# Rotating by partition-shifted ScalarE copies instead of permutation products

## The chip, the cores and the metric

The kernel runs on one core of a Trainium2 chip. The metric is device time in microseconds (us), lower is better. Before the change it takes 2796.73 us, the median of three runs (2792.71 to 2798.84).

## What is computed

A two-layer backbone with four parallel token mixers. It works on 512 latent and 256 context tokens, 1024 features, everything in float32. Each layer projects the normalised tokens to heads of four mixers (retention, gated linear attention, grouped-query attention, differential attention). Retention and grouped-query attention rotate their queries and keys, heads of 64 features, on the latent tokens only:

```
def apply_rope(x, cos, sin):
    h = x.shape[-1] // 2
    x1, x2 = x[..., :h], x[..., h:]
    return jnp.concatenate([x1 * cos - x2 * sin, x1 * sin + x2 * cos], axis=-1)

# retention:      q, k = apply_rope(z['ret_q']), apply_rope(z['ret_k']) * scale
# grouped-query:  q = apply_rope(rms_norm(z['gqa_q'], q_norm)); k = apply_rope(rms_norm(z['gqa_k'], k_norm))
```

The query heads of grouped-query attention are four, its key heads two. Differential attention rotates too, in heads of 32, and is not touched here.

## The kernel before

Features lie on the partitions and tokens along the free dimension. A "feature tile" is 128 features (two heads of 64) by up to 768 tokens; retention has four of them (queries 0 and 1, keys 2 and 3), grouped-query attention three (key tile 2 first, then query tiles 0 and 1). In layer 1 only the 512 latent tokens have queries. Values come from "token projections", with tokens on the partitions, two column tiles at a time for retention and one for grouped-query attention.

Each engine has its own list of instructions, written out by hand in order and joined by semaphores; `room` gives PSUM banks to products and makes TensorE (PE) wait until ScalarE (ACT) or VectorE (DVE) has freed them. A weight tile comes through a ring of four buffers; GpSimd (POOL) splits it into a high and a low part (L1284, L1287), and every product is three matmuls (L506 to L508 for feature and gate tiles, L547 to L549 for token projections).

Around a rotation this happens. PE projects feature tile n into banks (0,1) or (2,3), in turns. ACT copies it out to `q[:, n]` (`out_of_psum`, L1469, for retention; `queries_out`, L1510, with the norm weight, for the queries of grouped-query attention; L1633 for its keys), which frees the banks. PE then multiplies the tile by the 128x128 matrix `perm64`, which swaps the halves of each head and changes one sign (`rotate`, L668); that product is in plain float32 and shows as two matmul records. DVE multiplies the product by the sine table, the tile by the cosine table, and adds (`turn`, L1978, L1979, L1981). Retention has four rotations in each layer: two after the first token projection, two after the second. The first token projection of either mixer uses banks 0, 1 and 2, so it waits until ACT has freed the last feature tile. In grouped-query attention ACT also squares each tile for its norm (L1519) and that is what frees the banks; PE sums the squares (L653, L657), ACT takes the root (L1527, L1530), and DVE normalises the key tile (L1965 reciprocal, L1967) before it is rotated. At the end of that stage PE multiplies the rotated key tile by `swap`, which exchanges its two heads (`swapped_keys`, L924), and ACT copies the result to `q[:, 3]`, because query and key must lie on the same partitions.

In the retention stage of layer 0 ACT and DVE also build four "strips" of decays, one after each feature tile in ACT's order (`strip_exponentials`, L1388 to L1392). Strip h+1 begins on DVE only after strip h has ended there (L2014 to L2017, then L2006 and L2007), and each needs ACT's four exponentials in the middle.

Of the kernel before, what the change touches and what calls it, by code (L numbers as in the profile page):

```python
# [15 lines left out]
P = 128  # L16
# [3 lines left out]
T = LAT + CTX  # L20
# [28 lines left out]
SMALL = [("ident", P), ("ones", P), ("sum64", P), ("sum32", P), ("perm64", P), ("perm32", P),  # L49
         ("tri", 2 * P), ("rest", 2 * P), ("two", P), ("swap", P)]  # L50
# [4 lines left out]
def constants():  # L55

    f = np.float32
    j, i = np.arange(P)[:, None], np.arange(P)[None, :]
    c = {}
    c["ident"] = (j == i).astype(f)  # L60
    c["two"] = 2 * c["ident"]
    c["swap"] = (j == (i + P // 2) % P).astype(f)
    c["ones"] = np.full((P, P), 1.0 / D, f)
    for d in (64, 32):
        c[f"sum{d}"] = (j // d == i // d).astype(f) / d
        half = d // 2
        first = i % d < half
        c[f"perm{d}"] = (((j == i + half) & first) * -1.0 + ((j == i - half) & ~first) * 1.0).astype(f)
# [19 lines left out]
    rope = np.concatenate([*ret, *axial(64), *axial(32)], 1).astype(f)  # L88
    p = np.arange(P)[:, None]
    e = np.arange(7 * P)[None, :]  # L90
# [141 lines left out]
def bass_hybrid_backbone(nc, A, out, marks):  # L232
# [6 lines left out]
    with ctx:  # L239
# [215 lines left out]

        def query_roots(l, b, n):
            return q_scale[:, 0, n, 0:(4 if b == "dif" else 2) * NQ[l]]
# [24 lines left out]
        def _(pe):  # L482
# [177 lines left out]
            def rotate(l, b, n):  # L660
                key = ("rope", l, b, n)
                for s, c in room(key, 6 if n != feature_order(b)[-1] else 3 if b == "gqa" else 4):
# [254 lines left out]
            def swapped_keys(l):  # L917

                key = ("swap", l)
                for s, c in room(key, 4, 5):  # L920
                    pe.wait_ge(s, c)
                pe.wait_ge(*at(("turned", l, "gqa", 2)))
                for x, y in segs(T):
                    mm = pe.matmul(psum(key)[:, x:y], K["swap"], q[:, 2, x:y], start=True, stop=True)  # L924
                mm.then_inc(*up("pe_full", ("full", key)))

# [39 lines left out]
            for l in range(DEPTH):  # L966
# [27 lines left out]
                for b in ORDER:  # L994
                    nf, nt = len(BR[b]["feat"]), len(BR[b]["tok"])
                    lag = 4 if b == "ret" else 2
                    for j in range(nf + lag):
# [23 lines left out]
                        if b != "gla" and lag <= j < nf + lag - 1:  # L1021
                            rotate(l, b, feature_order(b)[j - lag])
# [326 lines left out]
        def _(act):  # L1349
# [156 lines left out]

            def queries_out(l, b, n):

                act.wait_ge(*at(("full", ("f", l, b, n))))
                act.activation(q[:, n, 0:W[l]], psum(("f", l, b, n))[:, 0:W[l]], ACT.Identity, scale=colv(l, 1, VB_QN + (0 if b == "gqa" else 2)),  # L1510
                               bias=zero).then_inc(*up("queries", ("turnable", l, b, n)))
# [107 lines left out]
            for l in range(DEPTH):  # L1619
                if l == 0:  # L1620
                    norm(l, 1)
                for b in ORDER:
                    nf, nt = len(BR[b]["feat"]), len(BR[b]["tok"])
                    for j in range(nf + nt):
                        if j < nf:
# [3 lines left out]
                            if b in ("gqa", "dif") and is_q(b, n):  # L1629
                                queries_out(l, b, n)  # L1630
                            elif b in ("gqa", "dif"):
# [38 lines left out]
                    if b == "gqa":  # L1670
                        out_of_psum(q[:, 3, :], ("swap", l), T)
# [77 lines left out]
        def _(dve):  # L1749
# [201 lines left out]
            def prep_tiles(l, b):  # L1951
# [17 lines left out]

                def turn(n):  # L1970
                    key = ("rope", l, b, n)
                    dve.wait_ge(*at(("free", ("f", l, b, n))))
                    dve.wait_ge(*at(("full", key)))
                    if b == "ret" and n == 0:
                        dve.wait_ge(*at(("rope_in", l)))
                    z = q[:, n, 0:LAT]
                    part = prep[:, 1, 0:LAT] if b == "ret" else prob[:, 0, 0, 0:LAT]
# [5 lines left out]
                if b == "ret":  # L1983
                    for n in range(tiles):
                        turn(n)
                    return
                keys, queries = feature_order(b)[:tiles - 2], feature_order(b)[tiles - 2:]
                for n in keys:
# [413 lines left out]
```

## Time and profile before

| what | value |
|---|---|
| median of three runs | 2796.73 us |
| span of the profiled execution | 2781.7 us |
| PE busy | 2638.2 us, 95% of the span |
| DVE, ACT, POOL busy | 47%, 26%, 53% |
| the chain that ended last | PE 83%, DVE 9%, ACT 3%, DMA 2% |
| mean granted TensorE clock | 0.981 of full speed |

The span is that of one execution under the profiler, from its first to its last instruction; what the device time has beyond it is start and end of the launch. The rows of a timeline give the start, the duration, the engine, the line of the kernel, the operation and its operands; "[1.30 <-DVE arena L1967]" says that the engine stood idle for 1.30 us before the row, until that instruction released it.

### The profile page before, as it was taken

To read this page: it belongs to the slowest core of one execution; us is meant where nothing else is said; L and a number is where in the kernel's file an instruction comes from. 1 tells how busy PE (TensorE), PEld (TensorE's weight loads), DVE (VectorE), ACT (ScalarE), POOL (GpSimd) and SP (SyncE) were. 2 spreads that over 40 slices of the span, in tenths; PEclk is the share of its full clock that TensorE was granted. 3 is DMA by queue.
4 is the path that set the end of the run, shared out by engine and by line. 5 is a ranking of instruction groups with operands and counts; after the bars stand their busy time and mean duration, and the time that the engine had idled before them with its cause. 6 is when DMAs were issued, how large, how long until landed. Compare 5 with 4: busy or idle time off the path is not lost.

```text
span 2781.7 us, 38375 instructions
## 1 busy us (share of the span) xinstructions
PE 2638.2 (95%) x15708; PEld 2172.5 (78%) x15708; DVE 1313.6 (47%) x1835; ACT 711.3 (26%) x1214; POOL 1465.5 (53%) x1375
## 2 busy tenths in 40 slices
PE   5999989998999999999999999998999889999999
PEld 2788878776877878888878888886777667888877
DVE  3622066534476847555573352317644667511231
ACT  4411143222254621111120121133321455211110
POOL 2543437521423526666669426545733436488886
PEclk9999989999999999999999999999999999999999
DMA  7522412211411834444433363221212218433322
GB/s 262 159 61 77 128 42 67 81 47 33 114 54 45 273 110 124 122 122 122 123 106 109 118 205 86 84 57 54 73 52 52 61 57 249 115 99 99 96 80 82
DMA packets 378083, 285.19 MB, mean 103 GB/s; under 512 B 10245, under 2 KB 338601, under 8 KB 377398
## 3 DMA queue, kind: packets, MB, share of 16 engines
q1 hardware_dynamic: 375680, 279.91, 33.7%
q8 instruction: 125, 2.05, 0.3%
q10 hardware_dynamic: 1622, 2.75, 0.3%
q14 instruction: 48, 0.39, 0.0%
q0 software_dynamic: 608, 0.09, 0.0%
HBM read 253.35 MB, written 29.36 MB: 102 GB/s over the span
## 4 chain that ended last, share of the span: by engine, by line
PE 83%; DVE 9%; ACT 3%; DMA 2%; issue 1%; POOL 1%; ACTq 0%; SPq 0%; DVEq 0%; POOLq 0%
PE ps L506 18%; PE ps L507 17%; PE ps L508 17%; PE ps L1137 3%; PE ps L678 3%; PE ps L547 2%; PE ps L549 2%; PE ps L548 2%; PE ps L1083 2%; DVE ffl L2328 2%; PE ps L762 2%; PE ps L782 1%; PE ps L889 1%; PE ps L640 1%; PE ps L709 1%
## 5 line engine op out<-in xcount | busy, mean ns | idle before, releaser
L1284 POOL TENSOR_TENSOR w_hi<-ring,tiny 128x512 fp32r<-128x512 f32 x484 | 535.5, 1106 | 1045.8 <-PE ps L508 612.2
L1287 POOL TENSOR_TENSOR w_lo<-ring,w_hi 128x512 fp32r<-128x512 f32 (+1 forms) x572 | 798.7, 1398 | 95.7 <-ACT w_hi L1489 57.5
L506 PE MATMUL ps<-hh,w_hi 128*128 128x512 f32 (+1 forms) x2288 | 836.7, 366 | 11.8 <-DVE hl L1906 9.8
L507 PE MATMUL ps<-hl,w_hi 128*128 128x512 f32 (+1 forms) x2288 | 812.9, 355 | 0.0
L508 PE MATMUL ps<-hh,w_lo 128*128 128x512 f32 (+1 forms) x2288 | 811.3, 355 | 0.0
L506 PEld LDWEIGHTS ps<-hh,w_hi 128*128 128x128 f32 x2288 | 438.6, 192 | 109.9 <-issue 29.1
L508 PEld LDWEIGHTS ps<-hh,w_lo 128*128 128x128 f32 x2288 | 438.4, 192 | 61.7
L507 PEld LDWEIGHTS ps<-hl,w_hi 128*128 128x128 f32 x2288 | 439.3, 192 | 57.5 <-issue 1.9
L547 PE MATMUL ps<-w_hi,hh 128*128 128x256 f32 (+1 forms) x544 | 156.8, 288 | 4.6 <-POOL w_lo L1287 2.5
L1557 ACT ACTIVATE arena<-ps,tiny,vec 128x768 f32<-128x768 f32 (+1 forms) x120 | 108.6, 905 | 197.5 <-DVE tiny L2064 197.4
L548 PE MATMUL ps<-w_lo,hh 128*128 128x256 f32 (+1 forms) x544 | 154.4, 284 | 0.0
L549 PE MATMUL ps<-w_hi,hl 128*128 128x256 f32 (+1 forms) x544 | 154.4, 284 | 0.0
L506 PE MATMUL ps<-ffh,w_hi 128*128 128x512 f32 x352 | 141.5, 402 | 11.6 <-DVE ffl L2328 11.5
L2337 DVE SCALAR_TENSOR_TENSOR arena<-ps,vec,arena 128x511 f32<-128x511 f32 x66 | 43.6, 661 | 224.0 <-ACT arena L1723 223.3
L1723 ACT ACTIVATE arena<-ps,vec 128x768 f32<-128x768 f32 (+1 forms) x44 | 39.0, 887 | 428.8 <-PE ps L508 428.8
L1834 DVE SCALAR_TENSOR_TENSOR rope<-ring,tiny,rope 128x1024 f32<-128x1024 f32 x84 | 146.4, 1783 | 0.7
L508 PE MATMUL ps<-ffh,w_lo 128*128 128x512 f32 x352 | 137.2, 390 | 0.0
L507 PE MATMUL ps<-ffl,w_hi 128*128 128x512 f32 x352 | 137.2, 390 | 0.0
L1469 ACT ACTIVATE arena<-ps 128x512 f32<-128x512 f32 (+3 forms) x116 | 65.1, 563 | 232.2 <-PE ps L508 231.1
L2063 DVE TENSOR_REDUCE tiny<-ps 128x1 f32<-128x768 f32 (+1 forms) x120 | 101.4, 845 | 44.3 <-PE ps L746 29.7
L1329 POOL TENSOR_TENSOR arena<-arena 128x128 f32<-128x128 f32 x140 | 60.8, 434 | 114.1 <-DVE xT L2166 68.4
L547 PEld LDWEIGHTS ps<-w_hi,hh 128*128 128x128 f32 x544 | 105.7, 194 | 10.4 <-issue 4.0
(256 smaller groups left out, 3837.0 us busy)
## 6 DMA issues: line engine op xcount, KB each, us to landing
ring<-in_w_in SPq DMA_DIRECT2D x118, 512.0 KB, 4.0
ring<-in_w_mod SPq DMA_DIRECT2D x96, 512.0 KB, 3.9
ring<-in_w_up SPq DMA_DIRECT2D x88, 512.0 KB, 4.1
ring<-in_w_down SPq DMA_DIRECT2D x48, 512.0 KB, 4.0
ring<-in_w_out SPq DMA_DIRECT2D x32, 512.0 KB, 4.1
logits<-arena SPq DMA_DIRECT2D x32, 384.0 KB, 2.3
arena<-logits SPq DMA_DIRECT2D x32, 384.0 KB, 4.5
ring<-in_w_down SPq DMA_DIRECT2D x24, 384.0 KB, 3.4
```

What stands on the lines that cost most here:

```text
L506: pe.matmul(acc, wh[:, offset + k], hi[:, n, x:y], start=n == 0, stop=False)
L507: pe.matmul(acc, wh[:, offset + k], lo[:, n, x:y], start=False, stop=False)
L508: mm = pe.matmul(acc, wl[:, offset + k], hi[:, n, x:y], start=False, stop=n == whole - 1)
L547: pe.matmul(to, hh[:, n, ts], wh[:, :, k], start=n == 0 and bank_begins, stop=False)
L548: pe.matmul(to, hh[:, n, ts], wl[:, :, k], start=False, stop=False)
L549: mm = pe.matmul(to, hl[:, n, ts], wh[:, :, k], start=False, stop=n == KT - 1 and bank_ends)
L678: mm = pe.matmul(psum(("oT", l, b, t))[64 * s:64 * s + 64, P * c:P * c + P], vt, pt[s][:, m], start=m == key_tiles(t)[0], stop=m == NT - 1)
L1284: pool.tensor_tensor(wh[:, 0:count], w, one[:].unsqueeze(2).to_broadcast([P, count, P]), ALU.mult).then_inc(*up("w_lead", ("lead", key, j)))
L1287: pool.tensor_tensor(wl[:, 0:count], w, wh[:, 0:count].bitcast(F32), ALU.subtract).then_inc(*up("w_split", ("split", key, j)))
L1557: act.activation(prob[:, h % 2, m, lo:T], psum(key)[:, lo:T], ACT.Exp, scale=scale, bias=nmx[:, c:c + 1], accum_out=rsum[t % 2][:, 4 * m + ...
L1834: ins = dve.scalar_tensor_tensor(out=mod_sum[:, s], in0=w, scalar=cs[:, s, k:k + 1], in1=mod_sum[:, s], op0=ALU.mult, op1=ALU.add)
L2063: link(dve.tensor_reduce(nmx[:, c:c + 1], acc[:, lo:T], AX, ALU.max))
```

## The change

The four rotations of retention and the three of grouped-query attention, in both layers, no longer use PE. ACT, when it takes a feature tile out of PSUM, writes it a second time with the 32-partition halves of each head exchanged: four activations of 32 partitions by 512 tokens, read from PSUM at one partition offset and written to SBUF at another. The sign goes into the sine table. For grouped-query attention the key tile is rotated before it is normalised (the root is the same for all features of a head), and its norm weight is applied by ACT. The head swap of the keys becomes two copies of 64 partitions by 768 tokens on ACT. The constant matrices `perm64` and `swap` are no longer loaded. Differential attention stays as it was.

```
+        def other_halves(l, b, n):
+            if b == "gqa":
+                return prob[:, n // 2, n % 2, 0:LAT]
+            if n == 3:
+                return q[:, 4, 0:LAT]
+            return (prep if l == 0 else pt_r).rearrange("p b t -> p (b t)")[:, n * LAT:(n + 1) * LAT]
...
             def rotate(l, b, n):
-                if b == "ret":
-                    pe.wait_ge(*at(("free", ("f", l, b, n))))
-                else:
-                    pe.wait_ge(*at(("turnable", l, b, n)))
-                pe.matmul(psum(key)[:, 0:LAT], K["perm32" if b == "dif" else "perm64"], q[:, n, 0:LAT],
+                pe.wait_ge(*at(("turnable", l, b, n)))
+                pe.matmul(psum(key)[:, 0:LAT], K["perm32"], q[:, n, 0:LAT],
                           start=True, stop=True).then_inc(*up("pe_full", ("full", key)))
...
-                        if b != "gla" and lag <= j < nf + lag - 1:
+                        if b == "dif" and lag <= j < nf + lag - 1:
                             rotate(l, b, feature_order(b)[j - lag])
...
-                    if b == "gqa":
-                        swapped_keys(l)
+                    if b == "dif":
+                        rotate(l, b, feature_order(b)[-1])
                     if b in ("gqa", "dif"):
-                        rotate(l, b, feature_order(b)[-1])
...
                     if b == "ret":
-                        rotate(l, b, nf - 1)
...
+            def halves_out(l, b, n, scale):
+                for to in range(0, P, 32):
+                    src = to ^ 32
+                    rows = slice(src, src + 32)
+                    ins = act.activation(other_halves(l, b, n)[to:to + 32], psum(("f", l, b, n))[rows, 0:LAT], ACT.Identity,
+                                         scale=scale[rows], bias=zero[rows])
+                return ins
...
             def queries_out(l, b, n):
...
+                ins = act.activation(q[:, n, 0:w], psum(("f", l, b, n))[:, 0:w], ACT.Identity, scale=column, bias=zero)
+                if b == "gqa":
+                    ins = halves_out(l, b, n, column)
+                ins.then_inc(*up("queries", ("turnable", l, b, n)))
+
+            def features_out(l, n):
+                key = ("f", l, "ret", n)
+                act.wait_ge(*at(("full", key)))
+                w = W[l] if is_q("ret", n) else T
+                act.activation(q[:, n, 0:w], psum(key)[:, 0:w], ACT.Copy)
+                halves_out(l, "ret", n, one).then_inc(*up("act_free", ("free", key)))
...
                     if b == "gqa":
-                        out_of_psum(q[:, 3, :], ("swap", l), T)
+                        act.wait_ge(*at(("turned", l, b, 2)))
+                        act.activation(q[0:64, 3, :], q[64:128, 2, :], ACT.Copy)
+                        act.activation(q[64:128, 3, :], q[0:64, 2, :], ACT.Copy).then_inc(*up("act_free", ("free", ("swap", l))))
...
+                def turn_halves(n):
+                    dve.wait_ge(*at(("free", ("f", l, b, n)) if b == "ret" else ("turnable", l, b, n)))
+                    if b == "ret" and n == 0:
+                        dve.wait_ge(*at(("rope_in", l)))
+                    z, part = q[:, n, 0:LAT], other_halves(l, b, n)
+                    dve.tensor_tensor(part, part, rope[:, cos_sin + 1], ALU.mult)
+                    link(dve.tensor_tensor(z, z, rope[:, cos_sin], ALU.mult))
+                    ins = dve.tensor_tensor(z, z, part, ALU.add)
+                    if b == "ret" or is_q(b, n):
+                        step(ins, "turned", ("turned", l, b, n))
+                        return
+                    link(ins)
+                    z, roots = q[:, n, 0:T], key_roots(n)
+                    dve.wait_ge(*at(("free", ("qkn", l, b, n))))
+                    link(dve.reciprocal(roots, roots))
+                    step(dve.tensor_tensor(z, z, roots, ALU.mult), "turned", ("turned", l, b, n))
```

## Rows read from the trace of the kernel before

**Rows 1.** The page, part 1: busy time, share of the span, instructions, by engine.

```profile
PE 2638.2 (95%) x15708; PEld 2172.5 (78%) x15708; DVE 1313.6 (47%) x1835; ACT 711.3 (26%) x1214; POOL 1465.5 (53%) x1375
```

**Rows 2.** Groups by shape, PE: count | busy us, mean ns | idle before.

```profile
L668 PE MATMUL ps<-arena,small 128*128 128x512 f32 x44 | 25.4, 661 | 9.2 <-DVE arena L1967 4.9 <-DVE arena L1978 1.8 <-ACT modv L1423 1.4
```

**Rows 3.** Timeline of PE, grouped-query stage of layer 0.

```profile
561.39 0.30 PE L547 MATMUL ps<-w_hi,hh 128*128 128x128 f32 x1
...
577.49 1.45 PE L653 MATMUL ps<-small,arena 128*128 128x2 f32 x12
578.80 1.10 PE L668 MATMUL ps<-arena,small 128*128 128x512 f32 x2
579.74 1.47 PE L938 MATMUL ps<-small,arena 128*128 128x128 f32 x12
581.05 1.46 PE L924 MATMUL ps<-arena,small 128*128 128x512 f32 x4
582.34 1.02 PE L668 MATMUL ps<-arena,small 128*128 128x512 f32 x2
...
588.76 1.56 PE L746 MATMUL ps<-arena 64*128 64x512 f32 x8
```

**Rows 4.** Groups by shape, ACT.

```profile
L1510 ACT ACTIVATE arena<-ps,tiny,vec 128x512 f32<-128x512 f32 x4 | 3.1, 777 | 17.5 <-PE ps L508 17.5
L1519 ACT ACTIVATE arena<-ps 128x512 f32<-128x512 f32 x4 | 2.3, 587 | 0.0
L1469 ACT ACTIVATE arena<-ps 32x768 f32<-32x768 f32 x2 | 1.6, 799 | 15.5 <-PE ps L508 15.5
```

**Rows 5.** Timeline of ACT, grouped-query stage of layer 0.

```profile
560.32 0.27 ACT L1527 ACTIVATE vec<-ps,tiny 128x12 f32<-128x12 f32 x1 [0.52 <-PE ps L653]
560.49 0.80 ACT L1519 ACTIVATE arena<-ps 128x768 f32<-128x768 f32 x1
```

**Rows 6.** Timeline of ACT, retention stage of layer 0.

```profile
94.89 0.95 ACT L1388 ACTIVATE arena<-arena 128x896 f32<-128x896 f32 x1 [3.40 <-DVE arena L2007]
...
108.60 0.91 ACT L1392 ACTIVATE arena<-dist,tiny 128x640 f32<-128x640 f32 x1
109.76 0.81 ACT L1469 ACTIVATE arena<-ps 128x768 f32<-128x768 f32 x1 [0.25 <-PE ps L508]
```

**Rows 7.** Timeline of PE, retention stage of layer 0.

```profile
112.63 0.35 PE L547 MATMUL ps<-w_hi,hh 128*128 128x256 f32 x1 [1.91 <-POOL w_lo L1287]
...
129.97 0.95 PE L577 MATMUL ps<-tiny,arena 128*128 128x2 f32 x8
...
166.52 0.71 PE L709 MATMUL ps<-arena 64*128 64x128 f32 x8
```

**Rows 8.** Timeline of PE, retention stage of layer 1.

```profile
1694.23 0.36 PE L547 MATMUL ps<-w_hi,hh 128*128 128x256 f32 x1 [0.95 <-ACT arena L1469]
...
1711.58 1.02 PE L668 MATMUL ps<-arena,small 128*128 128x512 f32 x2
...
1734.17 1.61 PE L709 MATMUL ps<-arena 64*128 64x128 f32 x24 [0.33 <-issue]
```

**Rows 9.** Timeline of PE, grouped-query stage of layer 1.

```profile
2014.77 0.95 PE L653 MATMUL ps<-small,arena 128*128 128x2 f32 x8
2017.02 1.10 PE L668 MATMUL ps<-arena,small 128*128 128x512 f32 x2 [1.30 <-DVE arena L1967]
```

**Rows 10.** Groups by shape, DVE.

```profile
L1965 DVE RECIPROCAL arena<-arena 128x768 f32<-128x768 f32 x6 | 29.7, 4953 | 45.4 <-ACT arena L1530 45.4
L1979 DVE TENSOR_TENSOR arena<-arena,rope 128x512 f32<-128x512 f32 x22 | 21.6, 981 | 0.0
```

**Rows 11.** Windows around the first rotations: length, PE, PEld, DVE, ACT, POOL busy, PEclk, DMA share, GB/s.

```profile
131.00:134.40 3.40, 1.85 (x2) 0.30 (x2) 0.00 (x0) 1.30 (x5) 3.24 (x4) 0.74 0.18 25
134.40:137.80 3.40, 2.64 (x6) 1.61 (x7) 2.42 (x4) 0.00 (x0) 0.54 (x1) 0.50 0.94 258
137.80:141.20 3.40, 3.40 (x24) 3.40 (x23) 1.55 (x3) 0.00 (x0) 0.00 (x0) 0.76 0.11 30
```

More of the change, by code:

```diff
@@ L48 @@
 VB_CW, VB_C, VB_QN, VB_ROWS = 0, 3 * FT, 3 * FT + 2 * KT, 3 * FT + 2 * KT + 4
-SMALL = [("ident", P), ("ones", P), ("sum64", P), ("sum32", P), ("perm64", P), ("perm32", P),
-         ("tri", 2 * P), ("rest", 2 * P), ("two", P), ("swap", P)]
+SMALL = [("ident", P), ("ones", P), ("sum64", P), ("sum32", P), ("perm32", P),
+         ("tri", 2 * P), ("rest", 2 * P), ("two", P)]
 W = {l: (T if l < DEPTH - 1 else LAT) for l in range(DEPTH)}
@@ L65, in constants @@
         c[f"sum{d}"] = (j // d == i // d).astype(f) / d
-        half = d // 2
-        first = i % d < half
-        c[f"perm{d}"] = (((j == i + half) & first) * -1.0 + ((j == i - half) & ~first) * 1.0).astype(f)
+    first = i % 32 < 16
+    c["perm32"] = (((j == i + 16) & first) * -1.0 + ((j == i - 16) & ~first) * 1.0).astype(f)
     c["tri"] = np.concatenate([(j <= i), (j >= i)], 1).astype(f) / 16
@@ L86, in axial @@
                                    (tok % GRID_W).astype(f)[:, None] * fr], -1), dim)
-    rope = np.concatenate([*ret, *axial(64), *axial(32)], 1).astype(f)
     p = np.arange(P)[:, None]
+    sign = np.where(p % 64 < 32, -1, 1).astype(f)
+    cos64, sin64 = axial(64)
+    rope = np.concatenate([ret[0], sign * ret[1], cos64, sign * sin64, *axial(32)], 1).astype(f)
     e = np.arange(7 * P)[None, :]
@@ L661, in rotate @@
                 key = ("rope", l, b, n)
-                for s, c in room(key, 6 if n != feature_order(b)[-1] else 3 if b == "gqa" else 4):
+                for s, c in room(key, 6 if n != feature_order(b)[-1] else 4):
                     pe.wait_ge(s, c)
-                if b == "ret":
-                    pe.wait_ge(*at(("free", ("f", l, b, n))))
-                else:
-                    pe.wait_ge(*at(("turnable", l, b, n)))
-                pe.matmul(psum(key)[:, 0:LAT], K["perm32" if b == "dif" else "perm64"], q[:, n, 0:LAT],
+                pe.wait_ge(*at(("turnable", l, b, n)))
+                pe.matmul(psum(key)[:, 0:LAT], K["perm32"], q[:, n, 0:LAT],
                           start=True, stop=True).then_inc(*up("pe_full", ("full", key)))
@@ L915, in gla @@
                     mm.then_inc(*up("pe_full", ("full", key)))
[L917 to L925, printed above, removed]
             def turn_outputs(l, b):
@@ L1505, in outputs_out @@
                     *up("act_free", ("free", key)))
+            def halves_out(l, b, n, scale):
[5 more added lines that the diff above has]
+                return ins
             def queries_out(l, b, n):
+                w = W[l] if is_q(b, n) else T
+                column = colv(l, 1, VB_QN + (0 if b == "gqa" else 2) + (0 if is_q(b, n) else 1))
                 act.wait_ge(*at(("full", ("f", l, b, n))))
-                act.activation(q[:, n, 0:W[l]], psum(("f", l, b, n))[:, 0:W[l]], ACT.Identity, scale=colv(l, 1, VB_QN + (0 if b == "gqa" else 2)),
-                               bias=zero).then_inc(*up("queries", ("turnable", l, b, n)))
+                ins = act.activation(q[:, n, 0:w], psum(("f", l, b, n))[:, 0:w], ACT.Identity, scale=column, bias=zero)
[8 more added lines that the diff above has]
+                halves_out(l, "ret", n, one).then_inc(*up("act_free", ("free", key)))
             def query_squares(l, b, n):
@@ L1628, in _ @@
                             M = 32 if BR[b]["feat"][n] == 2048 else P
-                            if b in ("gqa", "dif") and is_q(b, n):
+                            if b == "ret":
+                                features_out(l, n)
+                            elif b == "gqa" or (b == "dif" and is_q(b, n)):
                                 queries_out(l, b, n)
-                            elif b in ("gqa", "dif"):
+                            elif b == "dif":
                                 act.wait_ge(*at(("full", ("f", l, b, n))))
@@ L1973, in turn @@
                     dve.wait_ge(*at(("full", key)))
-                    if b == "ret" and n == 0:
-                        dve.wait_ge(*at(("rope_in", l)))
                     z = q[:, n, 0:LAT]
-                    part = prep[:, 1, 0:LAT] if b == "ret" else prob[:, 0, 0, 0:LAT]
+                    part = prob[:, 0, 0, 0:LAT]
                     dve.tensor_tensor(part, psum(key)[:, 0:LAT], rope[:, cos_sin + 1], ALU.mult).then_inc(*up("dve_free", ("free", key)))
@@ L1984, in prep_tiles @@
                     for n in range(tiles):
-                        turn(n)
+                        turn_halves(n)
                     return
                 keys, queries = feature_order(b)[:tiles - 2], feature_order(b)[tiles - 2:]
-                for n in keys:
+                for n in keys if b == "dif" else ():
                     if n != keys[0]:
```

4 lines of the change are left out of this document (3 added, 1 removed).

## The prediction

> **What bounds the kernel now.** I read the page first: PE is busy 95% of the span and the other engines at most 53% [rows 1], so work taken from PE is worth its time wherever PE goes on at once, and work given to ACT costs only where PE waits for ACT. Averages don't say where that is. So I read next PE's groups by shape, to count what goes, and then, for each of the four places where rotations stand (retention and grouped-query attention, layers 0 and 1), the timelines of PE, ACT and DVE side by side. There the reader should look at the row with which PE starts the first token projection: it needs the banks of the last feature tile, which ACT frees. In layer 1's retention PE already waits 0.95 us for exactly that ACT copy [rows 8]; in the grouped-query stage of layer 0 PE starts at 561.39, when ACT's last square (560.49 plus 0.80) has just ended [rows 3, 5]. Everything the change adds on ACT stands in front of that row. I take the sum against the profiled span of 2781.7 us; the median of the runs is 15.0 us more, and I leave those 15 as they are.
>
> **What goes from PE.** The rotations are 22, two records each [rows 2]; 8 of them are differential attention's and stay, 14 go. One takes 0.94 us from its start to the next product's (578.80 to 579.74), a key swap 1.29 (581.05 to 582.34) [rows 3]. That is 14 x 0.94 + 2 x 1.29 = 15.7 us (the second swap is taken at the same price). The waits around the rotations go with them.
>
> **What ACT gets.** One shifted copy is 512 tokens with a scale and a bias read from SBUF, the form of L1510: 777 ns against 587 for a plain one of that width [rows 4]. That it moves only 32 partitions saves nothing: a 32x768 copy takes 799 ns [rows 4]. An activation starts about 0.1 us before the one ahead ends (560.32 plus 0.27, next at 560.49) [rows 5]. So each copy costs 0.68 to 0.69 us in a queue and four cost 2.75 us per feature tile. The bounds: 0.49 us (the plain form, overlapped) and, if moving between partitions has a price that no row shows, anything above; that is a rival below. The same 2.75 us stand behind all 14 tiles, 38 us of ACT, but they are hidden behind the next projection of the same mixer, except after the last tile.
>
> **Retention, layer 0.** Two delays add up. The strips are a chain between ACT and DVE: ACT idles 3.40 us for DVE before the second strip's exponentials [rows 6], and DVE in turn waits for ACT, so four copies put in front of the first strip move the whole chain by 2.75. The third strip's last exponential ends at 109.51 now [rows 6], then at 112.3. Only then comes the last feature tile: one copy (0.71) and four halves (2.8) end at 115.8, and PE starts at 115.9 and not at 112.63 [rows 7], where it now waits for POOL's split: 3.3 us lost. After that come the gains. From the end of the first token projection to the first scores it is now 129.97 to 166.52, 36.55 us [rows 7]. What is left of it: the modulation product 0.95; the second projection, 144 matmuls like the first (17.34 us, so 0.120 each); the gate tile, 24 matmuls of 512 and 24 of 256 columns, 72 such units, 8.7. Together 27.0, gain 9.6. More than the four rotations (3.8), since their waits and a low clock go too (below). Net 6.3.
>
> **Retention, layer 1.** The last tile's halves add 2.75 to PE's wait. From 1711.58 to 1734.17 it is 22.6 us [rows 8]; left are 96 matmuls (11.6), 24 of 512 (5.8) and 0.33 of issue, 17.7: gain 4.9. Net 2.1.
>
> **Grouped-query, layer 0.** ACT's chain between the last query tile and its square has 0.52 us of waiting for PE in it [rows 5], which absorbs part of the 2.75: PE starts the token projection 2.2 later than 561.39. Behind it two rotations and the swap go, 0.94 + 1.29 + 0.94 = 3.2. Net 1.0.
>
> **Grouped-query, layer 1.** PE waits 1.30 us for DVE to normalise the keys, then rotates (2017.02), so the projection starts at 2017.96 [rows 9]. Afterwards ACT sets it: full at 2014.77 plus 0.2, copy 0.69, halves 2.75, root 0.17, square 0.59, handoff 0.1: 2019.3. Lost 1.3, gained the same 3.2. Net 1.9.
>
> **What costs nothing, and its cover.** DVE keeps three operations per tile (up to about 1 us each [rows 10]); it can do them while PE is still at the second token projection, which is over 11 us long, and before they stood behind PE. The key tile's reciprocal (4.95 us [rows 10]) moves behind the rotation and starts some 3 us later, but the scores come only at 588.76 [rows 3], more than 25 us after. The swap by ACT, two copies of 768 (about 1.6 us), stands behind the copies of the previous mixer's outputs; its cover is the half gate tile that PE does before the scores (2.7 us in layer 1, 5.4 in layer 0). By my count layer 1 has only some 0.2 us to spare, so up to 1 us could show there. In retention the gate tile's second half of weights is split by POOL only after the projection's last product; with the rotations gone, PE gets there 2.7 us after that product, and POOL's two operations are next to be late. No DMA is moved. SP stores gate logits after ACT's copies; in layer 1 these stand behind two tiles' halves and come some 5 us later, and the load queued behind the store waits with it, but that weight is used over 15 us later. The smaller table of constants is not what the start waits for: nothing, at most 0.5 us of gain.
>
> The four nets make 6.3 + 2.1 + 1.0 + 1.9 = 11.3 us.
>
> **The clock.** Around the first two rotations the granted clock is 0.50 for about 6.8 us (0.74, 0.50, 0.76 in three windows), after PE had done only small products and waits; that is 1.2 instead of 2.4 GHz. PE was busy 1.85, 2.64 and 3.40 us in them [rows 11], so it cost about 0.8 + 1.3 + 0.8 = 2.9 us. The change takes this away (it is inside the 9.6), but makes four new stretches in which PE has little or nothing: about 5 us before the projection in layer 0's retention, 4 in layer 1's, 5.6 and 4.5 us of tiny sums and waiting in the grouped-query stages. I count on the two long ones, at 2.2 each, between the 2.9 of all three windows and the 1.3 of the middle one alone: 4.4 us lost. The two ends are kept for the range.
>
> Forecast: 11.3 - 4.4 = 6.9 us, so the span about 2775 and the time 2790.
>
> **The rivals.**
> *All new gaps lower the clock, or ACT's delays are a little longer.* Four times 2.2 to 2.9 us is 8.8 to 11.6, which leaves 2.5 or nothing: 2794 to 2797. The Trainium skill, TensorE: Matmul & The Clock Gate, HAM oscillation, tells of a loop whose every idle gap throttled the engine again and was paid for each time; by it this rival would be the likeliest and the time about 2795. The trace agrees as far as one such gap goes, with PEclk at 0.50 behind it [rows 11]. For the rival: the gaps of 4 us are not much shorter than the others; the swap and POOL are close. Against it: PE waits of 1.9 us (112.63 [rows 7]) show no lowered clock in the trace.
> *No gap lowers it.* Gain 11 to 12.7, with copies at 0.6 us: 2784 to 2786. For it: PE works at full density up to three of the four. Against it: rows 11.
> *A shifted copy costs much more than a straight one.* The place is the same row in the four stages. With price p the lost time is 8p (two tiles in layer 0's retention) plus 4p three times, less about 4.4 absorbed: 20p - 4.4, against 20.9 won (9.6 + 4.9 + 3.2 + 3.2). It is slower by over 5.6 us once 20p is over 30.9, p over 1.55 us, 2.2 times the row's. At 1.7 us: 2805. Nothing in the trace moves data between partitions on ACT, so only the absence of a row speaks for it.
> *The change does not do what it says:* PE's idle time takes the place of the products fully, with everything else equal: 2796.7. Against it: the four gains lie behind the first token projection, where ACT has little to do.
>
> **How the numbers follow.** 0.2%, 5.6 us, is what a measurement of this kernel can tell from no change. Chances: forecast (two gaps, or one or three) 0.45; no gap 0.15; all gaps or longer ACT delays 0.25; no gain at all 0.06; expensive copies 0.09. The forecast's own range is 2787 to 2793, which crosses the limit at 2791.1; I give three quarters of it to faster. Faster: 0.34 + 0.15 + a little of the rest, 0.51. Slower: 0.09. Same: 0.40. Range for 8 in 10: from the no-gap case, 2784, to the end of the all-gaps case, 2797.
>
> **What would show it.** PE busy down by about 16 us; no L668 in retention and grouped-query stages; ACT busy up by 38 to 45. Four halves at 0.78 us each behind each tile's copy. PE's wait before the first token projection about 5, 3.7, 3.4 and 3.6 us, its releaser ACT. PEclk at 0.5 after the first and the third. Wrong if the halves take over 1 us, if PE waits elsewhere (for `turned`, the swap or POOL before the gate tile), or if the time saved in these stages is given back in the gated linear attention that follows.

## The result: slower, by two stages at half clock

The changed kernel takes 2808.9 us (median of 22 runs, 2802.7 to 2815.4), the kernel before 2798.9 in the same comparison (22 runs, 2773.4 to 2816.7): a ratio of 1.0046, 95% interval 1.0027 to 1.0065, so 10 us slower, beyond the 0.2% that the prediction took as its limit. Forecast were 2790 and a range from 2784 to 2797. The profiled execution has a span of 2813.4 us and a time of 2815.3; the first and last 1.9 us are all that lies around the span. So before's profiled span of 2781.7 stands for a run of some 2783.6, not for the median 15 us above it.

The page of the changed kernel, part 1, against [rows 1]:

```profile
PE 2662.6 (95%) x15672; PEld 2205.4 (78%) x15672; DVE 1318.3 (47%) x1835; ACT 759.5 (27%) x1272; POOL 1469.3 (52%) x1375
```

ACT has 48 us more in 58 more instructions. PE has 36 instructions fewer and is busy 24 us *longer*. That can't come from less work; something makes products slower. Groups by shape of the changed kernel show which (after the bar: busy us, mean ns, idle before):

```profile
L555 PE MATMUL ps<-w_hi,hh 128*128 128x256 f32 x448 | 130.3, 291 | 8.7 <-ACT arena L1505 7.2 <-ACT arena L1462 0.9 <-POOL w_lo L1280 0.5
...
L555 PE MATMUL ps<-w_hi,hh 128*128 128x128 f32 x96 | 39.9, 416 | 7.8 <-ACT arena L1533 7.8
```

The 128-column products of this line, which are grouped-query attention's token projection, take 416 ns on average, longer than those of twice the width. The timelines of PE and ACT in layer 0 show how it comes to that, against [rows 3, 5] (L555 to L557 are the old L547 to L549, L661 the old L653, L1533 the square, L1505 the shifted halves):

```profile
553.60 0.95 PE L585 MATMUL ps<-tiny,arena 128*128 128x2 f32 x8
554.41 1.48 PE L661 MATMUL ps<-small,arena 128*128 128x2 f32 x12
559.64 0.44 PE L555 MATMUL ps<-w_hi,hh 128*128 128x128 f32 x1 [3.75 <-ACT arena L1533]
...
590.39 2.66 PE L661 MATMUL ps<-small,arena 128*128 128x2 f32 x12
...
595.36 0.70 PE L514 MATMUL ps<-hh,w_hi 128*128 128x512 f32 x1
...
601.23 1.56 PE L751 MATMUL ps<-arena 64*128 64x512 f32 x8
```

```profile
553.80 0.99 ACT L1514 ACTIVATE arena<-ps,tiny,vec 128x768 f32<-128x768 f32 x1 [4.46 <-PE ps L516]
554.80 3.12 ACT L1505 ACTIVATE arena<-ps,tiny,vec 32x512 f32<-32x512 f32 x4
...
558.70 0.84 ACT L1533 ACTIVATE arena<-ps 128x768 f32<-128x768 f32 x1
```

ACT is where the prediction put it: copy, four halves, root, square, then PE may start. The wait is 3.75 us. But from 559.64 to 590.39 the projection takes 30.75 us, where before it took 16.1 [rows 3]. Windows over the same stretch (length, then PE, PEld, DVE, ACT, POOL busy, PEclk, DMA share, GB/s):

```profile
547.00:555.00 8.00, 8.00 (x56) 7.31 (x54) 6.19 (x3) 3.47 (x6) 6.14 (x6) 1.00 0.81 213
555.00:560.00 5.00, 1.25 (x10) 1.19 (x11) 4.45 (x7) 4.48 (x10) 2.17 (x2) 0.83 0.31 78
560.00:565.00 5.00, 5.00 (x25) 5.00 (x25) 1.61 (x3) 0.00 (x0) 0.00 (x0) 0.50 0.09 27
...
580.00:590.00 10.00, 10.00 (x49) 10.00 (x48) 0.00 (x0) 0.00 (x0) 0.00 (x0) 0.50 0.00 0
590.00:600.00 10.00, 10.00 (x46) 9.22 (x46) 0.58 (x3) 4.41 (x6) 2.31 (x2) 0.71 0.21 54
600.00:606.00 6.00, 6.00 (x40) 4.68 (x39) 2.25 (x4) 3.08 (x5) 1.36 (x2) 1.00 0.00 0
```

After 5 us in which PE worked 1.25, the granted clock is 0.50 (1.2 GHz), and it stays there through 30 us in which PE is busy without a pause, with the other engines idle. It is at 1.00 again only with the 512-column gate products behind, half a microsecond after their first at 595.36, so the small sums between them ran at half clock too (2.66 us against 1.45 in [rows 3]). Layer 1 is the same, by its timeline:

```profile
2027.23 0.95 PE L661 MATMUL ps<-small,arena 128*128 128x2 f32 x8
2032.23 0.44 PE L555 MATMUL ps<-w_hi,hh 128*128 128x128 f32 x1 [4.05 <-ACT arena L1533]
...
2062.98 1.81 PE L661 MATMUL ps<-small,arena 128*128 128x2 f32 x8
...
2071.10 1.56 PE L751 MATMUL ps<-arena 64*128 64x512 f32 x8
```

The two retention stages, for [rows 7, 8], PE's timeline (L714 are the scores):

```profile
114.22 0.35 PE L555 MATMUL ps<-w_hi,hh 128*128 128x256 f32 x1 [3.11 <-ACT arena L1505]
...
133.05 0.95 PE L585 MATMUL ps<-tiny,arena 128*128 128x2 f32 x8
...
159.75 0.82 PE L714 MATMUL ps<-arena 64*128 64x128 f32 x9
...
1709.57 0.55 PE L555 MATMUL ps<-w_hi,hh 128*128 128x256 f32 x1 [4.08 <-ACT arena L1505]
...
1729.48 0.28 PE L555 MATMUL ps<-w_hi,hh 128*128 128x256 f32 x1
...
1746.66 1.61 PE L714 MATMUL ps<-arena 64*128 64x128 f32 x24
```

And three rows more of the kernel before, PE's timeline: where layer 0's grouped-query projections end, where layer 1's token projection ends (the same sums as 2062.98 above), and its first scores:

```profile
557.99 0.95 PE L577 MATMUL ps<-tiny,arena 128*128 128x2 f32 x8
...
2033.98 1.00 PE L653 MATMUL ps<-small,arena 128*128 128x2 f32 x8
...
2041.66 1.56 PE L746 MATMUL ps<-arena 64*128 64x512 f32 x8
```

Step by step against before: layer 0's retention is 6.8 us earlier at its first scores (159.75, [rows 7] 166.52); at the last tile's sums of layer 0's grouped-query stage 4.4 of it are left (553.60 against 557.99); at its first scores the kernel is 12.5 late (601.23, [rows 3] 588.76), so this stage lost 16.9. Layer 1's retention ends 12.5 late, as it began (1746.66, [rows 8] 1734.17), and layer 1's grouped-query stage loses 17.0 again (29.4 us late behind it, by the same instructions in both traces). Two losses of 17 against one gain of 7. Of the 2.4 us that went between the two stages of layer 0, 1.6 lie before 366.13 (360.94 now), where a dip of the clock that both kernels have is longer in this run: the granted clock is 0.89 over the last 47.7 us before that row, 0.93 over the same work before. The remaining 0.8, and the 2.3 between 29.4 and the 31.7 us by which the spans differ, weren't traced.

Within the two grouped-query stages the 17 us split up like this. PE starts the token projection 2.6 us later in layer 0 and 1.9 in layer 1, counted from the last feature product. The projection loses 14.7 in each. Behind it, where the rotations and the swap have gone, layer 0 gains 0.4 (590.39 to 601.23, before 577.49 to 588.76) and layer 1 loses 0.4 (2062.98 to 2071.10, before 2033.98 to 2041.66).

### The profile page after: what moved, and what is told of

Read it like the earlier page. It is cut to its first block and busy times, and to the rows that moved or that the text cites. A ratio compares the mean times of both kernels' runs of the same rounds, so it can differ in the third digit from the quotient of the medians.

```text
span 2813.4 us, 38328 instructions
## 1 busy us (share of the span) xinstructions
PE 2662.6 (95%) x15672; PEld 2205.4 (78%) x15672; DVE 1318.3 (47%) x1835; ACT 759.5 (27%) x1272; POOL 1469.3 (52%) x1375
## 3 DMA queue, kind: packets, MB, share of 16 engines
q10 hardware_dynamic: 1622, 2.75, 0.3%
## 5 line engine op out<-in xcount | busy, mean ns | idle before, releaser
L514 PE MATMUL ps<-hh,w_hi 128*128 128x512 f32 (+1 forms) x2288 | 836.3, 366 | 12.5 <-DVE hl L1924 10.4
L555 PE MATMUL ps<-w_hi,hh 128*128 128x256 f32 (+1 forms) x544 | 170.2, 313 | 16.5 <-ACT arena L1533 8.0
L556 PE MATMUL ps<-w_lo,hh 128*128 128x256 f32 (+1 forms) x544 | 169.2, 311 | 0.0
L557 PE MATMUL ps<-w_hi,hl 128*128 128x256 f32 (+1 forms) x544 | 169.2, 311 | 0.0
L555 PEld LDWEIGHTS ps<-w_hi,hh 128*128 128x128 f32 x544 | 120.6, 222 | 20.7 <-ACT arena L1533 8.9
L556 PEld LDWEIGHTS ps<-w_lo,hh 128*128 128x128 f32 x544 | 120.6, 222 | 0.2 <-issue 0.2
```

Source lines behind the costliest of these rows:

```text
L514: pe.matmul(acc, wh[:, offset + k], hi[:, n, x:y], start=n == 0, stop=False)
L555: pe.matmul(to, hh[:, n, ts], wh[:, :, k], start=n == 0 and bank_begins, stop=False)
L556: pe.matmul(to, hh[:, n, ts], wl[:, :, k], start=False, stop=False)
L557: mm = pe.matmul(to, hl[:, n, ts], wh[:, :, k], start=False, stop=n == KT - 1 and bank_ends)
```

## The experiments

Twelve kernels ran. Theory A says that the low clock, once there, stays through the stream of 128-column products and costs 30.8 - 16.1 = 14.7 us per layer (the stream alone, without what runs at half clock behind it); theory B that the wait or ACT's and DVE's work beside it is the cost. Times are medians, and the ratio is to the kernel before on the same chip.

**Take the wait away.** The projection's 768 columns need two of the three banks that it asks for.

```diff
-for s, n in room(("tt", l, b, pair[0]), first, first + 1, first + 2):
+for s, n in room(("tt", l, b, pair[0]), *range(first, first + (3 if len(pair) == 2 else 2))):
```

> The changed kernel, but grouped-query attention's token projection (768 columns, so two banks) asks for two banks of the accumulator instead of three. Those two belong to the first feature tile, long read, so PE no longer waits for ACT after the last query tile (3.75 us in layer 0, 4.05 in layer 1 in the changed kernel's trace). Theory A (the wait lowers the clock, and the stream of 144 products of 128 columns then runs to its end at 0.50): PE starts at once after the small sums, the projection takes 16.1 us instead of 30.8 in both layers, and the kernel gains 2 x (3.8 + 14.7) = 37 us, or about 30 where the before kernel's level is shared by other losses: 2772 to 2780 us. Theory B (the wait is the whole cost, the slow projection has another cause, such as ACT's or DVE's traffic beside it): gain 7.8 us, about 2801, and the pitch stays at 0.21 us.

2778.8 us (2762.4 to 2788.8), ratio 0.9944 (0.9914 to 0.9974): 30 us under the changed kernel, far beyond theory B's 7.8. But its profile holds a surprise. Windows of layer 0, where PE had no wait at all (2.2 us of small sums from 547.06, then the projection from 549.22):

```profile
549.50:551.90 2.40, 2.40 (x24) 2.40 (x23) 2.37 (x3) 2.35 (x7) 1.22 (x1) 1.00 0.03 4
551.90:555.00 3.10, 3.10 (x17) 3.10 (x17) 2.56 (x7) 1.10 (x4) 0.00 (x0) 0.51 0.62 166
555.00:570.00 15.00, 15.00 (x72) 15.00 (x72) 0.10 (x1) 0.00 (x0) 2.31 (x2) 0.50 0.00 1
```

The clock falls just the same and stays down, but it falls inside the stream, 2.7 us after its start. In layer 1 of the same run it does not fall. So without the wait the clock is lost in some cases and not in others, which would explain the spread of 26 us. Whether the two-column products ahead of the stream bring it down or the stream itself does, this run can't tell; moving the sums (below) asks that.

**Keep PE busy in the wait.** Four plain products of 512 columns, whose output nothing reads, ahead of the wait:

```diff
+if b == "gqa" and pair[0] < 2:
+    for s, n in room(("fill", l), 6):
+        pe.wait_ge(s, n)
+    for i in range(4):
+        mm = pe.matmul(psum(("fill", l))[:, 0:512], K["ones"], rope[:, 4, 0:512], start=True, stop=True)
+    mm.then_inc(*up("pe_full", ("free", ("fill", l))))
 for s, n in room(("tt", l, b, pair[0]), first, first + 1, first + 2):
     pe.wait_ge(s, n)
```

> The changed kernel with four extra plain products of 512 columns per layer (0.94 us each by the rotations' rows), put ahead of the wait for ACT in front of grouped-query attention's token projection; their output is never read. The wait's end is set by ACT as before. Theory A (PE's idling in the wait lowers the clock and the projection keeps it low): PE is busy through the 3.8 us, the clock stays at 1.00, the projection takes 16.1 us: gain 2 x 14.7 = 29 us, 2778 to 2784 us, though PE does 7.5 us more work. Theory B (the wait, or ACT's and DVE's work beside the projection, is the cost): no gain, 2809 us or up to 4 more.

2775.5 us (2769.4 to 2780.9), ratio 0.9931 (0.9903 to 0.9959): 33 us less than the changed kernel for 7.5 us more work on the bounding engine. The expectation that the clock stays at 1.00 did not hold in layer 0. It fell, but the extra products took the dip, and the projection ran at full clock:

```profile
549.50:555.00 5.50, 5.50 (x14) 2.46 (x13) 4.92 (x9) 3.60 (x9) 1.38 (x1) 0.69 0.38 95
555.00:563.00 8.00, 8.00 (x74) 8.00 (x74) 0.26 (x1) 0.00 (x0) 0.11 (x1) 1.00 0.01 2
```

In layer 1 the clock stayed at 1.00 through the projection, as expected. Theory B can't have this: ACT's and DVE's work and what PE waits for are unchanged.

**The same products behind the wait** (the six lines moved under the room's wait).

> The same four extra products per layer, now behind the wait and in front of the token projection. The wait stays, and the clock falls in it as before. Theory A, in its form that only the 128-column products fail to raise the clock: the 512-column ones raise it within their own 4 to 7.5 us, the projection then takes 16.1 us: net gain per layer 14.7 less 3.8 to 7.5, so 14 to 22 us in all, 2787 to 2795. If a low clock lasts whatever PE does then, or if the cause lies beside PE: 8 to 15 us slower than the changed kernel, 2817 to 2824.

2787.8 us (2775.7 to 2790.5), ratio 0.9968 (0.9933 to 1.0003), 21 us less than the changed kernel. Timeline of PE and windows in layer 0:

```profile
558.48 5.97 PE L548 MATMUL ps<-rope,small 128*128 128x512 f32 x8 [3.74 <-ACT arena L1539]
563.88 0.62 PE L561 MATMUL ps<-w_hi,hh 128*128 128x128 f32 x1
```

```profile
554.50:558.50 4.00, 0.26 (x4) 0.20 (x3) 3.44 (x7) 3.82 (x9) 1.58 (x1) 0.72 0.31 66
558.50:564.00 5.50, 5.50 (x9) 2.42 (x9) 1.95 (x3) 0.00 (x0) 0.00 (x0) 0.58 0.16 47
564.00:572.00 8.00, 8.00 (x72) 7.76 (x71) 0.00 (x0) 0.00 (x0) 0.00 (x0) 1.00 0.01 2
```

The wait is the changed kernel's (3.74 us) and the clock falls in it. Four wide products at low clock cost 5.4 us and end the dip; 144 narrow ones don't. The wait alone is not the loss. With the clock kept, the stretch behind the projection takes 8.2 us in layer 0 and 4.9 in layer 1 of this run, 3.0 and 2.8 less than before (11.3 and 7.7), where the changed kernel gained 0.4 and lost 0.4. So half clock behind the projection costs that kernel a further 2.6 and 3.2 us.

**Is it the width?** Retention's token projection has 256-column products and came back to full clock after its own wait of 4.08 us. Here its first one is issued in halves of the width.

```diff
+for c in range(2):
+    half = to[:, c * P:(c + 1) * P]
+    pe.matmul(half, hh[:, n, ts], wh[:, c, k], ...)
+    pe.matmul(half, hh[:, n, ts], wl[:, c, k], ...)
+    mm = pe.matmul(half, hl[:, n, ts], wh[:, c, k], ...)
```

> The changed kernel with retention's first token projection issued in products of 128 columns instead of 256 (twice as many; the same sums). That asks whether the width is what keeps the clock low. At 0.112 us each 288 of them take 32 us instead of 17.3 at the full clock, so 15 us more per layer in any case. Theory A: in layer 1, where PE has waited 4.1 us for ACT, the granted clock stays at 0.50 to the end of the projection, about 60 us instead of some 35; the same in layer 0 if its wait of 3.1 us lowers the clock; 45 to 90 us over the changed kernel. If the width does not matter: 0.50 for 3 to 7 us as with 256 columns, and 29 to 36 us over it.

2903.7 us (one run), 95 over the changed kernel and 5 beyond the expected end. Windows of retention, first of the changed kernel (256 columns wide), two of layer 0 and two of layer 1:

```profile
114.20:117.00 2.80, 2.78 (x14) 2.80 (x15) 2.77 (x2) 0.54 (x1) 2.72 (x3) 0.56 0.76 217
120.00:124.00 4.00, 4.00 (x36) 4.00 (x35) 0.51 (x1) 3.43 (x4) 0.03 (x1) 1.00 0.75 171
...
1709.50:1715.00 5.50, 5.43 (x25) 5.46 (x26) 1.98 (x3) 0.00 (x0) 0.15 (x1) 0.50 0.63 160
1715.00:1720.00 5.00, 5.00 (x42) 5.00 (x41) 0.00 (x0) 0.00 (x0) 0.00 (x0) 0.96 0.00 0
```

And of this kernel's layer 0 (128 columns wide):

```profile
114.00:120.00 6.00, 5.90 (x29) 5.93 (x30) 5.89 (x5) 0.60 (x1) 5.84 (x4) 0.53 0.67 179
...
150.00:170.00 20.00, 20.00 (x95) 20.00 (x95) 0.00 (x0) 0.00 (x0) 0.00 (x0) 0.50 0.00 0
...
183.00:190.00 7.00, 7.00 (x61) 7.00 (x60) 0.00 (x0) 0.00 (x0) 1.43 (x2) 1.00 0.09 25
```

The same sums, the same stage, the same wait ahead (3.09 us in layer 0, 4.1 in layer 1): issued 256 wide the clock is back within 6 us, issued 128 wide it is at 0.50 for over 60 us, in both layers. It comes back in layer 0 with the second projection, which is 256 wide again. A product and its weight load take the same time at both widths (at half clock 0.213 us; at full clock 0.120 at 256 columns, 0.112 at 128), so products and weight loads per us are as many in either case, and PE shows as fully busy in both. What differs is the columns. In this pair the width decides whether the dip ends.

**Is the same loss in the kernel before?** The two-bank edit on it:

> The kernel before, with the same edit: grouped-query attention's token projection asks for two banks. In its profiled run PE started that projection right behind ACT's last square, at the full clock, and the run was 13 us under its median. Theory A with the addition that the other runs of before lose the clock in one of these two places: the median comes down by about 15 us plus 1 to 2 of removed wait, to 2780 to 2785. If nothing of the kind happens in before: 0 to 3 us faster than before.

2796.8 us (2779.5 to 2818.3), ratio 1.0020 (0.9984 to 1.0056): no gain, where 2780 to 2785 was expected, so the banks are not what costs before its 15 us. Its profiled run, 2818.3 us, has the low clock through both projections without a wait of PE for ACT. Hence a second look at the unchanged kernel:

> The kernel before, unchanged, for a second look at its profile. Theory A, as it stands: its time goes with the number of grouped-query token projections that run at 0.50. With none it is 2778 to 2787 us at a mean clock of 0.978 to 0.983, with one 2793 to 2805 at 0.971 to 0.977, with both 2808 to 2818 at 0.968 to 0.972. The trace must show the number that belongs to its time. If a run of some 2797 us has both projections at the full clock, the 15 us lie elsewhere, as the prediction had it.

2796.6 us, a typical run. Windows, first around layer 0's projection, then layer 1's:

```profile
565.00:575.00 10.00, 10.00 (x92) 10.00 (x92) 0.00 (x0) 0.00 (x0) 2.32 (x2) 1.00 0.01 2
```

```profile
2013.00:2018.00 5.00, 5.00 (x22) 4.38 (x20) 1.98 (x3) 0.00 (x0) 0.39 (x1) 0.50 0.41 105
2018.00:2033.00 15.00, 15.00 (x72) 15.00 (x72) 0.00 (x0) 0.00 (x0) 2.31 (x2) 0.50 0.01 1
```

One projection of two at 0.50, as the theory asks for that time (in this layer before's PE waits for DVE [rows 9], not for ACT). Of 64 runs of before in the later comparisons 20 lie from 2777 to 2788 us, 40 from 2793 to 2805, and 4 at 2808 to 2818: three groups some 15 us apart. The three profiles of such runs (2783.6 us with none at the low clock, 2796.6 with one, 2818.3 with both) fit them: mostly one projection at low clock, and which and how many differ from run to run of one program. That every run of a group has that number is inferred from its time and mean clock. In the changed kernel it is both in the profiled run, and by time and clock (2802.7 to 2815.4 us, 0.963 to 0.969) in all 22.

**Each mixer alone.** Retention by ACT's halves with grouped-query attention as before, and the reverse.

> The kernel before with retention alone changed to ACT's shifted halves; grouped-query attention keeps its rotations and the swap product. From the comparison of the two traces: 6.8 us gained in layer 0 and nothing in layer 1, so 5 to 7 us under before, with before's spread: median 2789 to 2792. If the change's loss is spread over both mixers: no gain, 2796 or more.

2790.1 us (2776.3 to 2794.1), ratio 0.9974 (0.9952 to 0.9996), gained as expected.

> The kernel before with grouped-query attention alone changed (ACT's halves, the swap by ACT); retention keeps its rotations. From the comparison of the two traces both layers lose 17 us against a run of before that keeps the clock (2780), so 2812 to 2816, 16 to 19 us over before's median, and with a spread under 15 us, since the clock is always lost. If the loss belonged to retention: like before or up to 4 us faster.

2813.7 us (2809.6 to 2818.3), ratio 1.0075 (1.0046 to 1.0104), with a spread of 9 us. The loss is in grouped-query attention.

**The fill in the kernel before**, to compare both kernels without the loss.

> The kernel before, with the four extra plain products ahead of grouped-query attention's token projection. In before they lie on PE's path (no wait of several us to hide them), so they cost up to 2 x 3.8 = 7.5 us, less what waits for ACT they cover (1 to 3). Theory A, with the loss in before being one of chance (mean clock of its runs between 0.981 and 0.969, times from 2778 to 2818; the profiled run of before with two banks has the low clock through both projections with no wait ahead of them): before is 2779 to 2785 where it loses nothing, and this kernel is 2782 to 2790 in all runs, 6 to 14 us faster than before's median and with a spread under 15 us. If before's spread has another origin: 2800 to 2804 with the same spread of 40 us.

2795.1 us (2789.5 to 2800.1), ratio 0.9991 (0.9972 to 1.0009). The spread of 26 to 40 us has shrunk to 10, as expected, but the level is 5 to 13 us above the expected one. The profiled run shows why. In layer 1 PE waits 1.30 us for DVE as before [rows 9], the clock falls there, and the four products run through most of the dip. Timeline of PE and windows:

```profile
2022.44 5.57 PE L538 MATMUL ps<-rope,small 128*128 128x512 f32 x8 [0.88 <-DVE arena L1984]
2027.44 0.62 PE L553 MATMUL ps<-w_hi,hh 128*128 128x128 f32 x1
```

```profile
2019.50:2022.40 2.90, 2.05 (x2) 0.48 (x2) 0.71 (x2) 0.00 (x0) 0.98 (x1) 0.50 0.25 50
2022.40:2027.40 5.00, 4.96 (x7) 2.20 (x8) 1.28 (x2) 0.00 (x0) 0.00 (x0) 0.62 0.26 76
2027.40:2034.00 6.60, 6.60 (x58) 6.34 (x57) 0.00 (x0) 0.00 (x0) 0.00 (x0) 1.00 0.00 0
```

The dip ends under the wide products, before the 128-column stream begins, as in the changed kernel with the fill. The fill and a new wait of 0.88 us for DVE ahead of it put the projection 4.2 us later in layer 0 and 7.4 in layer 1, 11.6 and not 7.5 in all, and 2783.6 plus 11.6 is the measured level. In the changed kernel the same products put it only 1.1 us later in layer 0 and not at all in layer 1; the rest hides in the waits. By ratios (0.9931 and 0.9991) the changed kernel with the fill is 17 us faster; less 11.6 and plus 1.1 leaves 6. Against the 12 runs of before under 2788 us in its own comparison (middle 2783.5) it is 8 us faster, 9 without its 1.1. So some 6 to 9 us are the change's own worth once grouped-query attention's clock is kept.

**A version faster than both.** First, in the changed kernel with two banks, the small sums go behind the token projection, so that it follows the wide products at once; then retention's token projections get banks whose tenants are long read.

```diff
-if b in ("gqa", "dif") and 1 <= j <= nf:
+if b in ("gqa", "dif") and 1 <= j <= nf and not (b == "gqa" and j == nf - 1):
     mean_squares(l, b, feature_order(b)[j - 1])
...
 token_projection(l, b, pair)
+if b == "gqa":
+    turned(b, nf - 1)
+    mean_squares(l, b, feature_order(b)[nf - 2])
```

> The two-bank kernel, with the small products (12 of two columns, and in layer 0 the 8 of the modulation's turning) that stood between the last feature projection and the token projection moved behind the token projection. Nothing light is left ahead of the 128-column stream. Theory A as it now stands (any light stretch ahead of that stream may trap it, wait or not: layer 0 of the profiled two-bank run has the low clock for 34 us with no wait): the clock stays at 1.00 in both layers in nearly all runs, 2762 to 2768 us, the level of the fastest runs of the two-bank kernel. If the stream of 128 columns falls to the low clock by itself: like the two-bank kernel, 2779, with the same spread.

2771.6 us (4 runs, 2767.7 to 2777.5), ratio 0.9910 (0.9879 to 0.9941). That is above the expected 2762 to 2768, and its interval overlaps that of the two-bank kernel (0.9914 to 0.9974); the spread is 10 us instead of 26, in 4 runs instead of 10. So that the sums bring the clock down is likely and not shown. Windows of layer 0: the whole projection at 1.00, and the dip now in the small sums behind it, where the gate tile's wide products end it:

```profile
544.00:560.00 16.00, 16.00 (x146) 16.00 (x145) 4.32 (x4) 3.73 (x5) 5.62 (x5) 1.00 0.13 34
560.00:567.00 7.00, 5.85 (x31) 5.79 (x31) 2.56 (x6) 2.55 (x8) 2.03 (x2) 0.53 0.28 75
```

```diff
-for s, n in room(("tt", l, b, pair[0]), first, first + 1, first + 2):
+banks = ((5, 6, 7) if pair[0] < 2 else (0, 1, 2)) if b == "ret" else range(first, first + (3 if len(pair) == 2 else 2))
+for s, n in room(("tt", l, b, pair[0]), *banks):
...
-return g if g < 4 else 6 if g in (5, 7) else 7
+return g if g < 4 else 4 if g == 5 else 6 if g == 7 else 7
```

> A candidate: the kernel with the small sums behind grouped-query attention's token projection, and besides it in retention the first token projection in banks 5 to 7 and the second in 0 to 2, so that neither waits for ACT's halves of the last feature tile (3.1 us in layer 0, 4.1 in layer 1 in the changed kernel's trace). Theory A: it gains the wait of both layers, less what then stands before the split weights (up to 1 us each), 5 to 7 us, and the clock of 0.50 behind them (about 2 to 3 us each): 2760 to 2765 us against 2771.6 of the kernel it starts from. If the ACT-bound chain only moves its wait behind the projection: 2768 to 2772.

2765.6 us (6 runs, 2753.6 to 2771.6), ratio 0.9895 (0.9864 to 0.9926), some 29 us under before. What the retention banks add to the moved sums (0.9910) is within the noise. Its waits of PE no longer have the 7.2 us for ACT ahead of retention's projections, but 2.3 for POOL's split weights:

```profile
PE ps L556 <- POOL w_lo L1285: 2.3, 2, 1.9
```

> The same retention banks with two banks for grouped-query attention's token projection, its small sums left in front of it, and the four extra plain products between them. It does 7.5 us more work than a kernel needs; theory A: no low clock in either projection, 2766 to 2773 with a spread under 15 us. Without the extra products it would be the two-bank kernel with its spread of 26 us.

2763.9 us (4 runs, 2761.7 to 2774.1), ratio 0.9903 (0.9870 to 0.9935), 2 us under the expected range: not told apart from the one without extra work.

## Why the prediction was wrong

**The failed step is the clock's: "I count on the two long ones, at 2.2 each ... 4.4 us lost".** That new gaps would lower the clock was right. Their number was not: the clock fell behind all four, as the rival of all gaps had it. The price failed most. It came from a dip behind which 512-column and 256-column products ran [rows 11]; in the grouped-query stages the stream behind the gap is 128 columns wide, and there the dip cost 14.7 us in the stream and some 3 more behind it, not 2.2, twice. With 1.5 and 2.6 us in the two retention stages the clock took 39 us instead of 4.4. The rival of all gaps had a cap of 2.9 us per gap, so no case of the clock reached the result. The Trainium skill, TensorE: Matmul & The Clock Gate, HAM oscillation, prices each gap as one transition to be paid again, by which I had "about 2795". The runs agree for 256 columns (6 us at 0.50 after 4.08 us of waiting) and not for 128 (over 60).

**"I leave those 15 as they are" was the second error.** The 15.0 us between before's span and its median were not around the span (1.9 us) but in it: a projection at low clock in most runs, and in neither layer of the profiled one. Part of what the change loses, before had lost already, which is why 10 us and not some 25 are missing.

**The four nets were nearly right.** Before the clock they measure 8.3, 2.3, 0.4 and 0.9, together 11.9 us, against 6.3, 2.1, 1.0 and 1.9, together 11.3. For the two grouped-query stages the gains behind the projection, 3.0 and 2.8 us, are taken from the kernel that kept its clock there (the fill behind the wait), since in the changed kernel the low clock covers them.

**ACT's price per half was too small, and cost little.** Predicted 2.75 us per tile by overlapping starts; measured 3.12 to 3.14, 0.78 from start to start. Alone one takes 773 ns, by the groups of the changed kernel, and the row it was priced by 777 [rows 4]:

```profile
L1505 ACT ACTIVATE arena<-ps,tiny 32x512 f32<-32x512 f32 x32 | 24.7, 773 | 0.4
```

So the rival of the expensive shifted copy is out. Why the four don't overlap is open. The waits came out at 3.11 (layer 0's retention), 4.08, 3.75 and 4.05 us against my 5, 3.7, 3.4 and 3.6.

**Retention, layer 0: net 6.8 instead of 6.3.** PE started at 114.22, 1.6 later and not 3.3. The prediction moved the whole chain of strips by the 2.75 us in front of it; in fact ACT's idle time for DVE shrank (2.06 us before the second strip, [rows 6] 3.40; 1.96 before the third, before 5.16), and the third strip began only 0.8 later. The projection then took 18.8 us instead of 17.3, since the clock was low at its start: 1.5 lost. Behind it (133.05 to 159.75, against 36.55) 9.9 came, predicted 9.6.

**Retention, layer 1: nothing instead of 2.1.** PE started 3.1 us late, and the 5.5 us at 0.50 made the projection 2.6 longer (1709.57 to 1729.48). Behind it 5.4 came, predicted 4.9. The clock's price of 2.2 to 2.9 was right here, where the products are 256 wide, and I had not counted it.

**What cost nothing did.** POOL's split takes nothing from the two gains in retention, and with the clock kept the swap by ACT (0.84 us per copy) and the later reciprocals leave 3.0 and 2.8 of 3.2 us. "Given back in the gated linear attention" did come in small: 1.6 us, by the longer dip there, which nothing ties to the change.

## What to carry to other kernels

Before putting work in front of a wait, look at what PE runs right behind it: here a dip of the clock cost 2 to 3 us when wide products followed and nearly as much as the whole stream again when narrow ones did, so put wide work, or none that waits, ahead of a narrow stream. When a kernel's runs fall in groups 15 us apart, one profile shows one group; compare the granted clock of its run with the others before taking its rows as the baseline. Here the mean granted clock of a run (0.981 for the profiled one of before, 0.971 to 0.977 for most others, 0.966 for the changed kernel) told which kind of run it was.

## What the hardware showed

- With uninterrupted PE work of 128x128 products of 128 columns, a granted clock that was at 0.50 stayed there for 30 us (0.213 us per product instead of 0.112), and for over 60 us in the narrow retention projection. With 256 columns it was back within 6 us, and 512-column products behind a wait ended it in 5.4. No run here shows the 128-column stream coming back by itself.
- Products of 128 and of 256 columns, each with its weight load, take the same 0.213 us at half clock, and 0.112 and 0.120 us at full clock. A full busy share of PE doesn't tell them apart, and the clock behaved differently under them.
- The clock can fall without any wait of PE: in the two-bank kernel it fell in layer 0, 2.7 us into the 128-column stream behind 2.2 us of two-column products, and not in layer 1 of the same run.
- ACT's copy of 32 partitions by 512 to other partitions, with scale and bias from SBUF, takes 773 ns, and one of 128 partitions in place 777.
